# Regrouping the turns of x at the head of a one-core decoder layer

## What is computed

```python
def block(x, ...):
    h = rmsnorm(x, g_mix_pre)
    p = h @ w_in                         # 2048 -> 4352 columns, in groups A, B, C
    ya, yb, yc = pool_mixer(...), short_conv_mixer(...), sgu_mixer(...)
    mix = concatenate([ya, yb, yc]) @ w_out
    x = x + rmsnorm(mix, g_mix_post)
    f = conv_ffn(rmsnorm(x, g_ffn_pre), ...)     # x @ ffn_up, gelu gate, @ ffn_down
    return x + rmsnorm(f, g_ffn_post)
```

## Time and profile before

| | |
|---|---|
| median of three runs | 1332.47 us (1332.05 to 1333.07) |
| profiled execution, its own time | 1332.47 us |
| its span, first to last instruction | 1330.8 us |
| TensorE matmuls busy | 1319.8 us (99%), 8970 instructions |
| VectorE, ScalarE, GpSimd busy | 798.7, 500.6, 73.2 us |
| read from HBM, written | 195.68 MB, 3.56 MB |

### The profile page before, as it was taken

One profiled execution on the slowest core, in us unless ns is written; L12 is line 12 of the kernel. 1 busy time (PEld: TensorE's weight loads), 2 busy tenths in 40 slices (PEclk: granted clock), 3 DMA queues, 4 the chain that ended last, 5 costly groups with the idle time before them and its releaser, 6 DMA issues.

```text
span 1330.8 us, 24552 instructions
## 1 busy us (share of the span) xinstructions
PE 1319.8 (99%) x8970; PEld 1312.0 (99%) x8970; DVE 798.7 (60%) x1256; ACT 500.6 (38%) x726; POOL 73.2 (5%) x186
## 2 busy tenths in 40 slices
PE   9999999999999999999999999999999999999997
PEld 8999999999999999999999999999999999999996
DVE  7758755544488655556655544555555455655875
ACT  7323333234464333323333332333333333333552
POOL 0051000000041000000000000000000000000000
PEclk9999999999999999999999999999999999999999
DMA  9754455565554554556455455645544565555453
GB/s 245 199 158 128 133 147 138 157 160 139 155 134 134 152 157 128 140 148 183 133 152 156 131 137 152 180 138 153 150 137 131 152 180 145 151 146 138 131 145 129
DMA packets 378792, 199.61 MB, mean 150 GB/s; under 512 B 4216, under 2 KB 375588, under 8 KB 378748
## 3 DMA queue, kind: packets, MB, share of 16 engines
q1 hardware_dynamic: 377940, 198.16, 54.2%
q10 hardware_dynamic: 736, 0.66, 0.2%
q0 software_dynamic: 80, 0.31, 0.1%
HBM read 195.68 MB, written 3.56 MB: 150 GB/s over the span
## 4 chain that ended last, share of the span: by engine, by line
PE 98%; DVE 1%; DMA 0%; issue 0%; SPq 0%; ACT 0%; DVEq 0%; ACTq 0%
PE mm L552 31%; PE mm L556 31%; PE mm L553 31%; DVE y_rows L1807 1%; PE tb L811 1%; PE tb L552 1%; PE tb L815 1%; PE tb L556 1%; PE tb L812 1%; PE tb L553 1%; PE tb L642 0%; DMA x_tok<-in_x_sample_dram 0%; PE tb L856 0%; PE tb L731 0%; PE mm L900 0%; PE mm L901 0%
## 5 line engine op out<-in xcount | busy, mean ns | idle before, releaser
L552 PE MATMUL mm<-a_hi,w_hi 128*128 128x320 f32 x1856 | 577.1, 311 | 0.2
L556 PE MATMUL mm<-a_lo,w_hi 128*128 128x320 f32 x1856 | 573.6, 309 | 0.0
L553 PE MATMUL mm<-a_hi,w_lo 128*128 128x320 f32 x1856 | 573.6, 309 | 0.0
L960 ACT ACTIVATE w_hi<-raw 128x1024 fp32r (+3 forms) x378 | 346.8, 965 | 441.7 <-PE mm L556 431.4
L1289 DVE TENSOR_TENSOR w_lo<-raw,w_hi 128x1024 fp32r<-128x1024 f32 (+1 forms) x376 | 409.5, 1130 | 112.9 <-ACT w_hi L960 112.2
L552 PEld LDWEIGHTS mm<-a_hi,w_hi 128*128 128x128 f32 x1856 | 348.5, 188 | 1.6 <-DVE w_lo L1330 0.5
L553 PEld LDWEIGHTS mm<-a_hi,w_lo 128*128 128x128 f32 x1856 | 348.5, 188 | 0.3
L556 PEld LDWEIGHTS mm<-a_lo,w_hi 128*128 128x128 f32 x1856 | 348.4, 188 | 0.0
L556 PE MATMUL mm<-m_lo,w_hi 128*128 128x320 f32 x884 | 273.2, 309 | 0.0
L552 PE MATMUL mm<-h_hi,w_hi 128*128 128x320 f32 x660 | 204.6, 310 | 0.0
L553 PE MATMUL mm<-h_hi,w_lo 128*128 128x320 f32 x660 | 204.0, 309 | 0.0
(11 more groups left out here) (277 smaller groups left out, 938.0 us busy)
## 6 DMA issues: line engine op xcount, KB each, us to landing
raw<-in_ffn_up_dram SPq DMA_DIRECT2D x88, 1024.0 KB, 5.8
raw<-in_ffn_down_dram SPq DMA_DIRECT2D x60, 704.0 KB, 4.8
raw<-in_w_in_dram SPq DMA_DIRECT2D x31, 1024.0 KB, 5.7
raw<-in_w_out_dram SPq DMA_DIRECT2D x16, 1024.0 KB, 6.0
raw<-in_ffn_down_dram SPq DMA_DIRECT2D x2, 1024.0 KB, 5.1
raw<-in_w_in_dram SPq DMA_DIRECT2D x3, 512.0 KB, 10.5
out_dram<-y_rows SPq DMA_DIRECT2D x6, 256.0 KB
x_tok<-in_x_prompt_dram SPq DMA_DIRECT2D x5, 256.0 KB, 4.3
```

Source lines behind the costliest of these rows:

```text
L552: pe.matmul(out, whi[:, s], hi, start=start, stop=False)
L553: pe.matmul(out, wlo[:, s], hi, start=False, stop=False)
L556: return pe.matmul(out, whi[:, s], tile(lo, k), start=False, stop=stop)
L960: act.activation(w_hi[:, d:d + half], src, ACT.Copy).then_inc(w_hi_done, 1)
```

## The change

In the order of TensorE the products of tile 0 come straight after the turn of tile 0. The turns of tiles 1 and 2 follow behind all six passes of tile 0, those of 3 and 4 behind tile 1, and from then on two tiles are turned in one group behind an odd tile: 5 and 6 behind tile 3, 7 and 8 behind 5, 9 and 10 behind 7, 11 and 12 behind 9, 13 and 14 behind 11, and 15 alone behind 13. One product on zeros is dropped. The turn of the sample tokens reads 64 rows and streams 64 columns. On ScalarE and VectorE weight part 1 is split ahead of `a_hi` and `a_lo` of tile 1 instead of behind them; the other parts stay behind those of their first tile.

```diff
                 for t0, nt in TT:
-                    last = pe.transpose(tb[k % 6][:, t0:t0 + P], x_tok[:, t0 // P, k * P:(k + 1) * P],
-                                        ident[:, :])
+                    last = pe.transpose(tb[k % 6][:, t0:t0 + nt], x_tok[0:nt, t0 // P, k * P:(k + 1) * P],
+                                        ident[0:nt, 0:nt])
                 last.then_inc(x_turned, 1)
...
-            AHEAD = 3
+            TURN_AFTER = {0: (1, 2), 1: (3, 4)}
+            TURN_AFTER.update({k: range(k + 2, min(k + 4, KD)) for k in range(3, KD - 2, 2)})
             keep_warm(2)
             turn_x(0)
-            keep_warm(1)
-            turn_x(1)
             keep_warm(1)
             for k in range(KD):
...
-                    if k == 0:
-                        turn_x(2 + e)
-                    elif e == 0 and k + AHEAD < KD:
-                        turn_x(k + AHEAD)
+                for t in TURN_AFTER.get(k, ()):
+                    turn_x(t)
...
             for k in range(KD):                      # ScalarE; the same on VectorE with a_lo
+                if k == 1:
+                    w_part(1)
...
-                if k and k in W_AFTER:
+                if k > 1 and k in W_AFTER:
                     w_part(W_AFTER.index(k))
```

## The result

| | before | after |
|---|---|---|
| median | 1332.52 us (1332.03 to 1333.99, 6 runs) | 1337.57 us (1337.1 to 1341.23, 6 runs) |
| ratio | | 1.0042, 95% interval 1.0032 to 1.0052 |
| profiled execution, time and span | 1332.47, 1330.8 | 1337.42, 1335.7 |
| stream goes on in chunk 2 (start of its second product, less a pass) | 27.28 | 32.21 |

The change makes the kernel 5.0 us slower, clear of noise. 1335.0 was forecast, with a range up to 1336.2: the direction is right, the size was missed by half, and the time lies outside the range.

The account below looks back on a forecast made before the run. TensorE's instruction stream, 98% of the chain of waits, was taken to bound the kernel; start -0.33, turns -0.72 and holes +3.6 gave +2.55 us, so 1335.0, range 1333.6 to 1336.2.

Parts of the forecast that it names:

- Edit 2: Sample turn on 64 rows and columns instead of 128: saves 0.04 us per turn, bounds 0 to 0.05, no loss.
- The slope of edit 2: A turn's price falls some 0.00065 us per streamed column, so 64 columns fewer save 0.04.
- Rival 2: The unpadded sample turn costs as much as a padded one: pairs at 0.65, sum +2.8, 1335.3 us; chance 0.23.
- Edit 1, grouping by itself: Turning two tiles in one group is worth about 0.01 us per pair, 0.1 in all.
- Edit 1, the lead: Later turns make TensorE wait for split weights: 0.2 us before tiles 2, 6, 10 and 0.8 before tile 12.
- Turn 15 and chunk 2: Turn 15 after tile 13 delays chunk 2's weight copy and split: wait of about 0.9 us before chunk 2.
- Edit 3: Tile 0's products ahead of turn 1: start 0.33 us earlier, then waits of 0.54, 0.19, 0.50, 0.19, each plus 0.10.
- Edit 4: Weight part 1 split first: no `w_lo` wait left for tile 1 (0.1 us before), at no cost.
- Rival 1: From tile 2 on ScalarE and VectorE keep up, waits are covered: 0.6 us faster, 1331.9; chance 0.06.
- rival 4: The sequence of turns changes only the last wait, turn 15 being late: +0.7, 1333.2 us; chance 0.06.
- Rival 3: TensorE's clock falls to its lower level from idling early in the head: 3 us more, 1338; chance 0.05.
- The sign of the whole: The whole change makes the kernel slower, by +2.55 us; chances: slower 0.47, same 0.50, faster 0.03.

Follow-up runs that it names:

- experiment 2: The kernel before with only the sample turn cut to 64 rows and columns; median 1337.93 us, ratio 1.0046.
- experiment 3: The changed kernel with each pair's four turns of 128 rows first and its two turns of 64 rows last; 1337.19 us.
- experiment 4: The changed kernel with the sample turn on 96 rows and 96 columns; 1335.21 us, ratio 1.0022.
- experiment 1: The changed kernel with the sample rows turned padded again, all else as changed; 1336.2 us, ratio 1.0029.
- experiment 8: The kernel before with tile 0's products ahead of turn 1 and weight part 1 split first, padded, later turns single; 1333.15 us, ratio 1.0005.
- experiment 5: The kernel of experiment 2 run twice more, unchanged; 1335.93 and 1340.49 us.

## Why the prediction was wrong, point by point

The prediction's sum was -0.33 for the start, -0.72 for the turns, +3.6 for the holes. By the trace of after it is -0.33; the turns 7 x 1.19 + 0.62 = 8.95 instead of 5.0, or +3.97; and holes of 2.1 instead of 0.8, or +1.3. These make 4.94, against 4.93 measured. The holes are the ones that the rows show: 0.15 where the stream starts, 0.23 and 0.24 at `a_lo` of tiles 0 and 1, 0.17 at `a_hi` of tile 1, 0.12 each at tiles 12 and 15, and 1.09 before chunk 2.

- **Edit 2 is the step that failed.** It was bounded by 0 to 0.05 saved per turn, with the sentence that a loss has no reason, since nothing is added to any instruction. The losing side was missing. A turn cost 0.28 more than a padded one (0.61 against 0.33, experiment 2), and the cost stands at no instruction but between two: the load of 64 rows behind turns of 128 rows is not made ahead of its product (experiment 3), and the load of 128 rows behind it comes late as well (0.21 instead of 0.11). The nearest rows had 88 to 128 rows, and the 96 rows of experiment 4 behave like them; the extrapolation went over an edge between 88 and 64. A product of few rows was in the trace of before, and the prediction did not use it: the product of 8 rows behind the head, here in weight loads, with the product L620 before it:

```profile
64.47 0.30 PEld L618 LDWEIGHTS tb<-diag,ones 128*128 128x128 f32 x2
64.69 0.30 PEld L620 LDWEIGHTS tb<-diag,ones 128*128 128x128 f32 x2
65.06 0.19 PEld L691 LDWEIGHTS tb<-ws,sel 8*64 8x64 f32 x2
65.30 0.19 PEld L552 LDWEIGHTS mm<-a_hi,w_hi 128*128 128x128 f32 x1
...
64.80 0.33 PE L620 MATMUL tb<-diag,ones 128*128 128x64 f32 x2
```

  The two loads of 128 rows at 64.47 are followed after 0.22; the two at 64.69 after 0.37, by the loads of 8 rows. One such row would have set a bound on the losing side: 0.15 at least for each change to few rows.
- **The slope of edit 2** held for half of the turns, with little at stake: 0.022 for 32 columns where another turn follows, nothing for the last turn of a group (experiment 4). For 64 columns it could not show, since the stops took more.
- **Rival 2** had the waits and padded price; experiment 1 is its case, with 29.80 for chunk 2 (30.1 with the start put right) and 1334.99 in the profiled execution (1336.2 in the median), against 1335.3. It had no part for the stops.
- **Edit 1, grouping by itself:** right. 0.65 for a padded pair, against 0.65.
- **Edit 1, the lead:** the mechanism is right and shown in experiment 1, where the four waits for `w_lo` and the last one stand where the steps had them. Its size in the changed kernel was 2.3 too large (holes of 2.1, not 4.4), and for a reason that was in the prediction's own terms: TensorE's arrival was counted with pairs of 0.57. With 1.19 it arrives at 1.19 + 1.76 + 1.19 = 4.14 after a group's start instead of 2.90, later than the chain's 3.10, and the waits before tiles 2, 6 and 10 vanish; that before tile 12 shrinks to 0.1. So half of the unexpected 4.7 us of turns went into waits that were expected.
- **Turn 15 and chunk 2:** right. The hole before chunk 2 was 1.09 against 1.03 forecast; it has no turn between it and its cause, so nothing covered it.
- **Edit 3:** right in what it meets. `a_lo` is waited for by tiles 0 and 1 as forecast (0.23 and 0.24 with their restart against 0.29). The 0.50 and restart forecast for `a_hi` of tile 1 are 0.17 in the changed kernel, where the slow turns cover them, and 0.62 with padded ones (9.37 - 7.95 - 0.147 - 0.65 in experiment 1); alone, it is no measurable gain (experiment 8).
- **Edit 4:** right, no wait on weight part 1 is left.
- **Rival 1** (the lead suffices) and **rival 4** (turn 15 alone is late) fall with experiment 1. **Rival 3**, the clock, is not what happened in the profiled execution of after; experiment 5 shows a relative of it, a clock that rises late instead of falling, at a price of 4.5, not 3.
- **The sign of the whole** was right, and not by luck alone: without the stops (experiments 1 and 4) the kernel is still slower, by the waits that were forecast. The chance of 0.47 for slower was too small, because the one unknown operation of the change was given no losing side.

## What to carry to other kernels

An operation whose shape is not in the trace has no price until a row of that shape is found: bound it on both sides, look for the row with the fewest rows or columns anywhere in the run, and put the edge cases into the sum as losses. In this kernel a stream of products of 128 rows should not be broken by single products of 64 rows; side by side they pay the change once (0.89 a pair instead of 1.19), though here waits took most of that back. Before turns are moved later to group them, count the chain from turn to the last thing queued behind it (here the split of the next chunk's weights), and compare it with TensorE's arrival.

## What the runs showed of the hardware

- A weight load of 64 rows behind loads of 128 rows waits 0.17 us with TensorE's queue naming no engine, and going there and back costs about 0.3 us. One of 96 rows does not wait (0.64 per pair against 0.66 with 128), nor does one of 88; one of 8 rows comes 0.15 late.
- In a group of turns the next start comes after 0.108 us with 128 streamed columns, after 0.086 with 96 (experiment 4) and after some 0.08 with 88 to 92, each with 128 loaded columns.
- TensorE's clock rose to its upper level (2.4 GHz) at 4.85 to 6.38 us in ten of the twelve traces, at 10.71 in experiment 8's and at 17.58 in one of experiment 5's. There a pass took 0.27 before and 0.15 behind, and the late rise cost 4.56 us of 1336, nearly as much as the whole change. Ahead of the rise the granted clock of the views reads 1.00, since the trace has no entry there.
